# The stripe order of projected columns: in the matmul's access patterns, or when PSUM is emptied

## What is computed

```python
h = rms_norm(x, pre_g)
proj = h @ w_in                      # 12 parts of 1536 columns, 3 gates of 2048
o_a = dilated_mixture_attn(q_a, k_a, v_a) * silu(z_a)
o_c = b_c * causal_short_conv(c_c * u_c, conv_w, conv_b) * silu(z_c)
o_r = retention(q_r, k_r, v_r) * silu(z_r)      # rotary on q and k; rows normalised per head
merged = sigmoid(g_a) * (o_a @ w_branch_a) + sigmoid(g_c) * (o_c @ w_branch_c) \
       + sigmoid(g_r) * (o_r @ w_branch_r)
x = x + rms_norm(merged @ w_out, post_g)
```

## Time and profile before

| what | value |
|---|---|
| median of 3 runs | 2778.6 us (2778.03 to 2779.01) |
| the profiled execution, its own time | 2779.1 us |
| its span, first to last instruction | 2777.1 us |
| PE busy | 2757.6 us, 12192 matmuls |
| PE weight loads (beside the matmuls) | 2254.8 us |
| DVE busy | 1777.7 us |
| ACT busy | 1266.8 us |
| POOL busy | 28.1 us |
| mean granted TensorE clock | 0.999 |
| mean DMA rate | 209 GB/s |

### The profile page before, as it was taken

One profiled execution on the slowest core, in us unless ns is written; L12 is line 12 of the kernel. 1 busy time (PEld: TensorE's weight loads), 2 busy tenths in 40 slices (PEclk: granted clock), 3 DMA queues, 4 the chain that ended last, 5 costly groups with the idle time before them and its releaser, 6 DMA issues.

```text
span 2777.1 us, 30124 instructions
## 1 busy us (share of the span) xinstructions
PE 2757.6 (99%) x12192; PEld 2254.8 (81%) x12192; DVE 1777.7 (64%) x2000; ACT 1266.8 (46%) x1462; POOL 28.1 (1%) x36
## 2 busy tenths in 40 slices
PE   9999999999999999999999999999999999999998
PEld 7888888888888888888878888888888888888887
DVE  6656764555675666578576567645656756666784
ACT  6454543444453334354454545434444533344543
POOL 0000000000000000000000000000000000000000
PEclk9999999999999999999999999999999999999999
DMA  9667465666566676666576674656665656766663
GB/s 333 206 218 227 159 227 190 217 207 212 182 227 197 212 222 202 214 211 214 182 231 201 215 232 152 231 194 212 211 214 180 229 192 202 235 204 213 209 214 121
DMA packets 299291, 579.76 MB, mean 209 GB/s; under 512 B 12304, under 2 KB 37264, under 8 KB 298896
## 3 DMA queue, kind: packets, MB, share of 16 engines
q1 hardware_dynamic: 260976, 517.50, 56.3%
q10 hardware_dynamic: 37168, 55.13, 6.8%
q0 software_dynamic: 1008, 5.20, 0.6%
HBM read 548.43 MB, written 29.36 MB: 208 GB/s over the span
## 4 chain that ended last, share of the span: by engine, by line
PE 94%; DVE 3%; ACT 1%; DMA 1%; issue 0%; POOL 0%; ACTq 0%; DVEq 0%; SPq 0%; POOLq 0%
PE ps L898 30%; PE ps L899 30%; PE ps L900 30%; DVE w_trail L1233 1%; PE ps L852 1%; PE ps L853 1%; PE ps L851 1%; DVE raw L1243 1%; ACT w_lead L972 1%; DMA bounce_z<-z_sb 1%; PE ps L795 0%; PE ps L797 0%; PE ps L794 0%; PE ps L773 0%; PE ps L777 0%
## 5 line engine op out<-in xcount | busy, mean ns | idle before, releaser
L1233 DVE TENSOR_TENSOR w_trail<-raw,w_lead 128x1024 fp32r<-128x1024 f32 x1009 | 1228.0, 1223 | 948.8 <-ACT w_lead L972 945.6
L972 ACT ACTIVATE w_lead<-raw 128x1024 fp32r<-128x1024 f32 x1009 | 1061.9, 1059 | 1375.8 <-PE ps L900 1274.2
L898 PE MATMUL ps<-w_lead,hT_lead 128*128 128x512 f32 x3136 | 1238.7, 395 | 9.6 <-DVE w_trail L1233 6.7
L900 PE MATMUL ps<-w_lead,hT_trail 128*128 128x512 f32 x3136 | 1233.6, 393 | 0.0
L899 PE MATMUL ps<-w_trail,hT_lead 128*128 128x512 f32 x3136 | 1233.5, 393 | 0.0
L898 PEld LDWEIGHTS ps<-w_lead,hT_lead 128*128 128x128 f32 x3136 | 589.2, 188 | 150.2 <-DVE w_trail L1233 11.4
L900 PEld LDWEIGHTS ps<-w_lead,hT_trail 128*128 128x128 f32 x3136 | 589.1, 188 | 135.1
L899 PEld LDWEIGHTS ps<-w_trail,hT_lead 128*128 128x128 f32 x3136 | 589.3, 188 | 132.9
L898 PE MATMUL ps<-w_lead,oT_lead 128*128 128x512 f32 x576 | 224.2, 389 | 0.0
L900 PE MATMUL ps<-w_lead,oT_trail 128*128 128x512 f32 x576 | 224.1, 389 | 0.0
L899 PE MATMUL ps<-w_trail,oT_lead 128*128 128x512 f32 x576 | 224.1, 389 | 0.0
(11 more groups left out here) (125 smaller groups left out, 1048.8 us busy)
## 6 DMA issues: line engine op xcount, KB each, us to landing
raw<-w_in SPq DMA_DIRECT2D x381, 1024.0 KB, 5.2
raw<-w_out SPq DMA_DIRECT2D x32, 1024.0 KB, 5.1
raw<-w_branch_a SPq DMA_DIRECT2D x24, 1024.0 KB, 5.7
raw<-w_branch_c SPq DMA_DIRECT2D x24, 1024.0 KB, 5.2
raw<-w_branch_r SPq DMA_DIRECT2D x24, 1024.0 KB, 5.7
bounce_q<-vq_sb ACTq DMA_DIRECT2D x18, 512.0 KB, 3.3
vq_sb<-bounce_q ACTq DMA_DIRECT2D x72, 128.0 KB, 3.5
bounce_z<-z_sb ACTq DMA_DIRECT2D x18, 512.0 KB, 3.2
```

What stands on the lines that cost most here:

```text
L898: pe.matmul(acc, lead[:, k, tok(t)], wl, start=opens, stop=False)
L900: last = pe.matmul(acc, trail[:, k, tok(t)], wl, start=False, stop=closes)
L972: act.activation(w_lead[:, (l * HALVES + h) % SPLIT_SLOTS, :], raw[:, SLOT_OF[l, i][0], part:part + HALF * COLS], ACT.Copy).then_inc(lead_ ...
L1233: dve.tensor_tensor(w_trail[:, s, :], raw[:, SLOT_OF[l, i][0], part:part + HALF * COLS], w_lead[:, s, :].bitcast(F32), ALU.subtract).then_ ...
```

## The change

It moves the stripe order from the matmul to the reading of the bank. The matmul reads the weights in one run of 512 columns and writes the bank in plain (h, j, a) order for every block. ACT and DVE then read the bank through `cut`, which is now a pattern of 16 runs of 32, and write the striped tile through `quads`. Rotary of retention now works on heads with plain tables, cos, sin and neg_sin of 64 columns per tile, broadcast over the heads (the constants shrink from 1968 to 1328 columns). Where z and c are emptied, the row scale is left out and the operation becomes a tensor_tensor; the missing factor comes in later: u and b of conv take `x_sq`, the square of `x_rstd`, attention's `row_inv` and retention's `o_rstd` are multiplied by `x_rstd`. Rotary keeps its four instructions a tile (two sin parts, the cos part, the sum). In the diff, `rotate`, `sums` and the evictions of z and c are DVE's; `rstd` is POOL's. The scratch of the software-driven DMAs is 4096 instead of 2048 bytes.

```diff
-            def columns_out(n, ap):
-                kind, mixer, role, _j = BLOCKS[n][3]
-                if kind == "mix" and role != "v":
-                    return ap.rearrange("p (j h a) -> p j h a", h=HPB, j=QUADS)
-                return ap
-            def columns(n, ap):
-                kind, mixer, role, _j = BLOCKS[n][3]
-                if kind == "mix" and role != "v":
-                    return ap.rearrange("p (h j a) -> p j h a", h=HPB, j=QUADS)
-                return ap
...
-                    wl = columns(n, w_lead[:, slot, i * COLS:(i + 1) * COLS])
-                    wt = columns(n, w_trail[:, slot, i * COLS:(i + 1) * COLS])
+                    wl = w_lead[:, slot, i * COLS:(i + 1) * COLS]
+                    wt = w_trail[:, slot, i * COLS:(i + 1) * COLS]
                     for t in tiles:
-                        acc = columns_out(n, bank(n, t)[:, :])
+                        acc = bank(n, t)[:, :]
...
         def quads(tile, t):
-            return by_quad(tile)[:, :, t].rearrange("p j h a -> p j (h a)")
+            return by_quad(tile)[:, :, t]
         def cut(ap):
-            return ap.rearrange("p (j c) -> p j c", j=QUADS)
+            return ap.rearrange("p (h j a) -> p j h a", h=HPB, j=QUADS)
...
                             if role in "qkub":
+                                scale = x_sq if mixer == "conv" else x_rstd
                                 act.activation(quads(copy_to, t), cut(bank(n, t)[:, :]), ACT.Copy,
-                                               scale=x_rstd[:, t:t + 1]).then_inc(evicted[n % 2], 1)
+                                               scale=scale[:, t:t + 1]).then_inc(evicted[n % 2], 1)
...
                 if kind == "mix" and role == "z":
-                        dve.scalar_tensor_tensor(quads(z_sb, t), cut(bank(n, t)[:, :]), x_rstd[:, t:t + 1],
-                                                 quads(z_sb, t), ALU.mult, ALU.mult).then_inc(evicted[n % 2], 1)
+                        dve.tensor_tensor(quads(z_sb, t), cut(bank(n, t)[:, :]), quads(z_sb, t),
+                                          ALU.mult).then_inc(evicted[n % 2], 1)
                 elif kind == "mix" and role == "c":
-                        dve.scalar_tensor_tensor(quads(q_sb, t), cut(bank(n, t)[:, :]), x_rstd[:, t:t + 1],
-                                                 quads(v_sb, t), ALU.mult, ALU.mult).then_inc(evicted[n % 2], 1)
+                        dve.tensor_tensor(quads(q_sb, t), cut(bank(n, t)[:, :]), quads(v_sb, t),
+                                          ALU.mult).then_inc(evicted[n % 2], 1)
...
-                        dve.scalar_tensor_tensor(sin_part[:, s, :], src[:, 1 - s, :], (x_neg, x_rstd)[s][:, t:t + 1],
-                                                 rope["sin"][:, t, :], ALU.mult, ALU.mult)
+                        table = rope["neg_sin" if s == 0 else "sin"][:, t, :]
+                        dve.scalar_tensor_tensor(sin_part[:, :, s, :], src[:, :, 1 - s, :], x_rstd[:, t:t + 1],
+                                                 table.unsqueeze(1).to_broadcast((P, HPB, 64)),
+                                                 ALU.mult, ALU.mult)
...
-                pool.tensor_scalar(x_neg, x_rstd, -1.0, 0.0, ALU.mult, ALU.add).then_inc(x_rstd_ready, 1)
+                pool.tensor_tensor(x_sq, x_rstd, x_rstd, ALU.mult).then_inc(x_rstd_ready, 1)
                 for g in range(GROUPS):
                     wait(o_ssq_ready, l * GROUPS + (g + 1))
-                    rstd(o_ssq, o_mean, l * GROUPS + (g + 1), o_rstd, P, 8).then_inc(o_rstd_ready, 1)
+                    rstd(o_ssq, o_mean, l * GROUPS + (g + 1), o_rstd, P, 8).then_inc(o_pow, 1)
+                    pool.wait_ge(o_pow, l * GROUPS + (g + 1))
+                    pool.tensor_tensor(by_tile, by_tile, x_rstd.unsqueeze(1).to_broadcast((P, HPB, TILES)),
+                                       ALU.mult).then_inc(o_rstd_ready, 1)
...
                 elif what == "sums":
                     dve.reciprocal(row_inv, row_sum).then_inc(inv_ready, 1)
+                    dve.wait_ge(inv_ready, 2 * (l * GROUPS + g) + 1)
+                    dve.tensor_tensor(row_inv.rearrange("p (h t) -> p h t", t=TILES),
+                                      row_inv.rearrange("p (h t) -> p h t", t=TILES),
+                                      x_rstd.unsqueeze(1).to_broadcast((P, HPB, TILES)), ALU.mult).then_inc(inv_ready, 1)
...
-    nc = bacc.Bacc("TRN2", target_bir_lowering=False, num_devices=1, dynamic_dma_scratch_size=2048)
+    nc = bacc.Bacc("TRN2", target_bir_lowering=False, num_devices=1, dynamic_dma_scratch_size=4096)
```

More of the change, by code:

```diff
@@ L54 @@
 PAIRED_GATES = {"attention": (2,), "conv": (2,), "retention": (2,)}
-CONST_PARTS = (("ident", P), ("log_count", 3 * P), ("causal", 3 * P), ("cos", TILES * COLS // 2),
-               ("sin", TILES * COLS // 2), ("gamma_q", TILES * HEADS),
+CONST_PARTS = (("ident", P), ("log_count", 3 * P), ("causal", 3 * P), ("cos", TILES * 64),
+               ("sin", TILES * 64), ("neg_sin", TILES * 64), ("gamma_q", TILES * HEADS),
                ("gamma_v", TILES * HEADS))
@@ L416, in build @@
         gamma_v = const("gamma_v").rearrange("p (h t) -> p h t", t=TILES)
-        rope = {n: const(n).rearrange("p (t f) -> p t f", t=TILES) for n in ("cos", "sin")}
+        rope = {n: const(n).rearrange("p (t f) -> p t f", t=TILES) for n in ("cos", "sin", "neg_sin")}
         xT_sb = merged[:, :, :].rearrange("p t c -> p (t c)").rearrange("p (k s) -> p k s", s=SEQ)
@@ L429, in conv_bias @@
             return tap(l, 3, ch)
-        x_ssq, x_sum, x_rstd, x_neg = stat[:, 56:64], stat[:, 0:2], stat[:, 2:4], stat[:, 4:6]
+        x_ssq, x_sum, x_rstd, x_sq = stat[:, 56:64], stat[:, 0:2], stat[:, 2:4], stat[:, 4:6]
         y_sum, y_rstd = stat[:, 12:14], stat[:, 14:16]
@@ L491, in build @@
         o_mean = sem("o_mean")
+        o_pow = sem("o_pow")
         o_rstd_ready = sem("o_rstd_ready")
@@ L737, in _ @@
                 pool.wait_ge(x_pow, l + 1)
-                pool.tensor_scalar(x_neg, x_rstd, -1.0, 0.0, ALU.mult, ALU.add).then_inc(x_rstd_ready, 1)
+                pool.tensor_tensor(x_sq, x_rstd, x_rstd, ALU.mult).then_inc(x_rstd_ready, 1)
                 for g in range(GROUPS):
                     wait(o_ssq_ready, l * GROUPS + (g + 1))
-                    rstd(o_ssq, o_mean, l * GROUPS + (g + 1), o_rstd, P, 8).then_inc(o_rstd_ready, 1)
+                    rstd(o_ssq, o_mean, l * GROUPS + (g + 1), o_rstd, P, 8).then_inc(o_pow, 1)
+                    pool.wait_ge(o_pow, l * GROUPS + (g + 1))
+                    by_tile = o_rstd.rearrange("p (h t) -> p h t", t=TILES)
+                    pool.tensor_tensor(by_tile, by_tile, x_rstd.unsqueeze(1).to_broadcast((P, HPB, TILES)),
+                                       ALU.mult).then_inc(o_rstd_ready, 1)
                 pool.dma_start(post_gain, post_g[l:l + 1, :].to_broadcast((P, D_MODEL))).then_inc(post_gain_in, 16)
@@ L1288, in rotate @@
                 for t in range(TILES):
-                    src = bank(n, t)[:, :].rearrange("p (s c) -> p s c", s=2)
-                    sin_part = work2[:, 1, :].rearrange("p (s c) -> p s c", s=2)
+                    src = bank(n, t)[:, :].rearrange("p (h s f) -> p h s f", h=HPB, s=2)
+                    sin_part = work2[:, 1, :].rearrange("p (h s f) -> p h s f", h=HPB, s=2)
                     if t > 0:
@@ L1294, in rotate @@
                     for s in range(2):
-                        dve.scalar_tensor_tensor(sin_part[:, s, :], src[:, 1 - s, :], (x_neg, x_rstd)[s][:, t:t + 1],
-                                                 rope["sin"][:, t, :], ALU.mult, ALU.mult)
-                    cos = rope["cos"][:, t, :].unsqueeze(1).to_broadcast((P, 2, COLS // 2))
-                    dve.scalar_tensor_tensor(work2[:, 0, :].rearrange("p (s c) -> p s c", s=2), src,
-                                             x_rstd[:, t:t + 1], cos, ALU.mult, ALU.mult).then_inc(evicted[n % 2], 1)
+                        table = rope["neg_sin" if s == 0 else "sin"][:, t, :]
+                        dve.scalar_tensor_tensor(sin_part[:, :, s, :], src[:, :, 1 - s, :], x_rstd[:, t:t + 1],
+                                                 table.unsqueeze(1).to_broadcast((P, HPB, 64)),
+                                                 ALU.mult, ALU.mult)
+                    cos = rope["cos"][:, t, :].unsqueeze(1).to_broadcast((P, 2 * HPB, 64))
+                    dve.scalar_tensor_tensor(
+                        work2[:, 0, :].rearrange("p (h f) -> p h f", f=64),
+                        bank(n, t)[:, :].rearrange("p (h f) -> p h f", f=64), x_rstd[:, t:t + 1], cos,
+                        ALU.mult, ALU.mult).then_inc(evicted[n % 2], 1)
                     dve.wait_ge(evicted[n % 2], l * (TILES * NBLOCKS // 2) + (TILES * (n // 2 + 1) + t + 1))
@@ L1410, in side_work @@
                     dve.reciprocal(row_inv, row_sum).then_inc(inv_ready, 1)
+                    dve.wait_ge(inv_ready, 2 * (l * GROUPS + g) + 1)
```

(10 more changed lines are left out.)

## The result

The changed kernel takes 2740.82 us (median of 4, 2740.45 to 2741.14), the kernel before 2778.81 beside it (2778.03 to 2779.41): ratio 0.9863, 95% interval 0.9846 to 0.9881. It is 1.4% faster, as forecast. A second set of runs, with the last experiment, gave 2739.54 and 2779.3, ratio 0.9860 (0.9843 to 0.9876).

A forecast was written before the change was run, and what follows sets the result against it. PE was taken as the bound, through its matmul start-to-start distance. 38.4 us gained in matmul order, less 0.1 at the start and 0.6 in third retention groups, gave 37.7 less: 2740.9 us, 8-in-10 range 2738 to 2745.5.

The forecast's parts named there:

- The bound: Whole kernel: PE's matmul start-to-start distance sets the time; splits by ACT and DVE keep up when PE is 2.9% faster.
- The order in the matmul: 30 mixer blocks a layer other than v: 5760 matmuls go from 233.33 to 226.67 ns, 38.4 us less.
- What the prediction left open: Striped matmuls: whether reading the operand or writing PSUM costs the 6.66 ns; said not to matter.
- The evictions, nothing: ACT and DVE emptying banks in 16 runs of 32: no added time, all under PE's work.
- the lower end: Bank evictions: reading PSUM in runs of 32 costs nothing, argued from line 1420; the end taken.
- the upper one: Bank evictions: each run costs an instruction's fixed part, 4.9 us a tile on ACT, 3.9 on DVE.
- the straight line through 342 and 744 ns: DVE evictions: fixed part 208 ns plus 1.05 ns an element, used to argue that runs of 32 cost nothing.
- The scales: z and c on DVE go from 744 to 682 ns, 48 times: 3 us less DVE work, under PE.
- The 0.6 us charged to the third retention groups: Retention's extra POOL multiplication delays gating 0.3 us; charged fully to PE's paired gates once a layer, after ACT's bounce.
- The first rival: Third retention group: bounce sharing queues with post_gain lands 2 to 3 us later; 4 to 6 us lost, 2745 to 2747; 7%.
- The third rival's threshold: 42 striped-eviction blocks: PE stands for delay beyond 5.8 us lead; 6.7 us more a block turns the sign; rival 2850, 2%.
- The total: Whole kernel: 37.7 us less, median 2778.6 to 2740.9 us, 1.4% faster; forecast given 86%.

The follow-up runs named there:

- the last experiment: The changed kernel run once more, unaltered, to check small differences: 2739.54 us, ratio 0.9860 to the kernel before.
- The two runs that exchange order and side work: Kernel before, moving operand read plainly and bank written in runs: 2740.51 us; changed kernel, both walked in 16 runs of 32: 2778.16 us.
- The first experiment: Kernel before, but moving operand read in one run of 512 and bank written in 16 runs of 32: 2740.51 us, ratio 0.9862.
- the control: The changed kernel run once more, unaltered, on another chip: 2739.54 us.

## Why the prediction was right, step by step

**The bound.** PE stayed at 99% and the mean distance in conv is 226.7 ns: as said. ACT and DVE had room: from 443.1 to 702 us DVE works 149.30 and ACT 113.36 of 258.90 us, 58% and 44%, where 58% and 43% were forecast.

**The order in the matmul, 38.4 us.** 268.80 - 261.12 = 7.68 us in conv's first stretch of 1152 matmuls, 6.67 ns each, is what the sum took for all 5760. The two runs that exchange order and side work show this as the cause. What the prediction left open, read or write, is settled for this order: the read alone.

The Trainium skill's page "Advanced Engine Details and Errata", Memory Cachelines, which the prediction weighed, comes out half and half. For PSUM it says that every two consecutive elements should be contiguous for best throughput. The first experiment agrees (16 runs of 32, 389 ns). For PSUM it also says that any pattern that is not contiguous slows matmuls significantly. The first experiment doesn't agree, and neither do the runs with 64 and 128. The prediction had set this sentence on PSUM beside a price that lay in the read of SBUF. For SBUF the page says that accesses which stay in one line of 16 bytes have full performance. By that, reading in runs of 32 would be free, and it costs 2.9% of the matmul; the runs with 16 and 8, in which the write is broken too, cost 2.1 and 5.5% on average. The measurement decides.

**The evictions, nothing.** 677 ns as before: the lower end that I took was exact, the upper one (4.9 us) far off. The reason that the prediction gave was weak, though: the straight line through 342 and 744 ns was drawn through the very row that it was to explain, so that this row lies on it says nothing about runs. The scales: 683 ns against a forecast of 682, POOL's extra instruction 0.20 us.

**What the sum had wrong.** The 0.6 us charged to the third retention groups is neither shown nor refuted by the change itself. PE's waits behind them, both layers together, were 1.76 us before (0.96 and 0.80). With the change they were 2.61 in one trace and 1.86 in the control's, so 0.85 or 0.10 more:

```profile
1172.45 0.47 PE L893 MATMUL ps<-w_lead,hT_lead 128*128 128x512 f32 x1 [0.20 <-DVE w_trail L1229]
...
1179.14 0.50 PE L893 MATMUL ps<-w_lead,hT_lead 128*128 128x512 f32 x1 [0.99 <-DVE w_trail L1229]
...
2537.40 0.47 PE L893 MATMUL ps<-w_lead,hT_lead 128*128 128x512 f32 x1 [0.45 <-DVE w_trail L1229]
...
2544.09 0.50 PE L893 MATMUL ps<-w_lead,hT_lead 128*128 128x512 f32 x1 [0.97 <-DVE w_trail L1229]
```

The reason given for it doesn't hold: with the same result delayed by another 1.3 us they were 1.74. I had taken a delay ahead of a contended transfer to pass through it in full. The term was small enough not to matter for the number. The first rival named the right place (a bounce that shares the queues with post_gain), but the change lost at most a microsecond there, and some 2 us were to be gained there by starting that load later.

**The third rival's threshold.** I had said that PE loses nothing up to 5.8 us of delay a block, and that 6.7 us would undo the gain. At 2.8 us a block it lost 5.3 us already, and at some 6.9 us 110, nearly three times the gain, where the rival's rule gives 42 x (6.9 - 5.8) = 46. The lead of a split at its start isn't the cover of a stage: other side work uses the same lead at the same time, and after the longest wait PE's clock was at its lower level for 4.8 us. The judgement (2%) stands, since the price was nothing; its arithmetic was too kind by more than a factor of two.

The total, 37.7 less for 2740.9, met 2740.8 and in the second set 2739.5. That it met the first within 0.1 us is luck: two sets differ by 1.3.

## What to carry to other kernels

These points rest on this one kernel. When PE is the bound, compare the start-to-start distance of equal matmuls between stages, not their busy share: a few ns on thousands of instructions were 1.4% here, under a busy figure of 99% in both kernels. Put a reordering where it was free here in runs of 32, in the write of PSUM or in the reading by ACT and DVE, and not in the read of the moving operand, unless its runs are as long as the 64 or 128 columns that were free here; the smallest edit that did this took two lines and gave the whole gain. And before a delay is charged in full, look whether what follows is a transfer that shares the queues with another: its end may not move with its start.

## What the runs showed of the hardware that was not expected

- A matmul of 512 fp32r columns whose moving operand is read in 16 runs of 32 starts its successor 6.66 ns later than one with a single run (233.3 for 226.7 ns), with the write of the bank plain. With read and write both in runs it is 6.66 or 9.9 ns for 16 runs of 32, by the order of the runs, 4.8 on average for 32 runs of 16, and nothing measurable for runs of 64 or 128 (2740.21 and 2739.69 us against 2740.8). The price doesn't grow steadily with the number of runs.
- With 64 runs of 8 the same instructions are 233.3 ns apart in most blocks, as with 16 runs of 32, and 263.3 in k and z of attention's second and third groups, in both layers. Why is open.
- The write of a bank in runs of 32 (2740.51 us, 389 ns), and its reading in such runs by ACT (677 ns) and DVE (683 ns), cost nothing.
